# Taking twelve matmuls whose results nobody reads out of the routing of a mixture of experts

## The reference

```
def moe_ffn(h, router_w, w1, w3, w2):
    logits = (h @ router_w).astype(jnp.float32)
    vals, idx = lax.top_k(logits, TOP_K_EXPERTS)
    probs = jax.nn.softmax(vals, axis=-1)
    gate = jnp.sum(jax.nn.one_hot(idx, N_EXPERTS, dtype=jnp.float32) * probs[..., None], axis=-2)
    gate = gate.astype(h.dtype)
    out = jnp.zeros_like(h)
    for e in range(N_EXPERTS):
        out = out + gate[..., e:e + 1] * swiglu(h, w1[e], w3[e], w2[e])
    return out
```

## Time and profile before

| what | value |
|---|---|
| median of 3 runs | 1699.44 us (1698.66 to 1702.03) |
| the profiled execution's own time | 1701.22 us |
| its span | 1699.4 us |
| mean granted TensorE clock of the span | 0.988 |
| TensorE busy | 1638.2 us (96%), 8944 matmuls |
| VectorE busy | 1373.6 us (81%) |
| ScalarE busy | 1072.0 us (63%) |
| HBM read | 473.40 MB, 283 GB/s over the span |

### The profile page before, as it was taken

One profiled execution on the slowest core, in us unless ns is written; L12 is line 12 of the kernel. 1 busy time (PEld: TensorE's weight loads), 2 busy tenths in 40 slices (PEclk: granted clock), 3 DMA queues, 4 the chain that ended last, 5 costly groups with the idle time before them and its releaser, 6 DMA issues.

```text
span 1699.4 us, 24355 instructions
## 1 busy us (share of the span) xinstructions
PE 1638.2 (96%) x8944; PEld 1389.6 (82%) x8944; DVE 1373.6 (81%) x1140; ACT 1072.0 (63%) x896; POOL 458.4 (27%) x541
## 2 busy tenths in 40 slices
PE   7899998999999999999999999999999999999998
PEld 5787888989989788878888888888888888888786
DVE  6999675455669976688888888888888888888887
ACT  6345455444455554577777777777777777777774
POOL 8996801999142541233000000000000000000100
PEclk9899999999999999999999999999999999999999
DMA  8343555556544455489999999999999999999994
GB/s 315 122 156 120 173 192 189 186 168 227 166 151 149 149 162 176 139 300 391 369 378 378 370 367 388 365 386 382 365 374 378 373 385 376 360 380 370 385 395 180
DMA packets 212460, 481.58 MB, mean 283 GB/s; under 512 B 7936, under 2 KB 32640, under 8 KB 212144
## 3 DMA queue, kind: packets, MB, share of 16 engines
q1 hardware_dynamic: 207456, 463.34, 76.3%
q0 software_dynamic: 4512, 16.78, 2.7%
q10 hardware_dynamic: 432, 0.65, 0.1%
HBM read 473.40 MB, written 7.34 MB: 283 GB/s over the span
## 4 chain that ended last, share of the span: by engine, by line
PE 65%; DVE 4%; ACT 1%; DMA 1%; issue 1%; DVEq 0%; ACTq 0%
PE ps L649 19%; PE ps L651 19%; PE ps L650 19%; PE ps L1257 1%; DVE w_lo L281 1%; DMA raw<-moe_w 1%; PE ps L673 1%; PE ps L674 1%; PE ps L675 1%; PE ps L848 0%; ACT w_hi L276 0%; PE ps L1305 0%; DVE hid L2331 0%; DVE x_tok L2545 0%; PE ps L1210 0%
## 5 line engine op out<-in xcount | busy, mean ns | idle before, releaser
L281 DVE TENSOR_TENSOR w_lo<-raw,w_hi 128x2048 fp32r<-128x2048 f32 (+1 forms) x439 | 1013.1, 2318 | 239.2 <-ACT w_hi L276 237.7
L276 ACT ACTIVATE w_hi<-raw 128x2048 fp32r<-128x2048 f32 (+1 forms) x439 | 840.0, 1915 | 378.1 <-PE ps L651 285.7
L649 PE MATMUL ps<-w_hi,xg_hi 128*128 128x512 f32 x896 | 355.4, 397 | 0.8 <-DVE w_lo L281 0.8
L651 PE MATMUL ps<-w_hi,xg_lo 128*128 128x512 f32 x896 | 349.6, 390 | 0.0
L650 PE MATMUL ps<-w_lo,xg_hi 128*128 128x512 f32 x896 | 348.9, 389 | 0.0
L649 PE MATMUL ps<-w_hi,hidT_hi 128*128 128x512 f32 x528 | 207.5, 393 | 3.4 <-DVE hidT_lo L2345 1.8
L651 PE MATMUL ps<-w_hi,hidT_lo 128*128 128x512 f32 x528 | 206.4, 391 | 0.0
L650 PE MATMUL ps<-w_lo,hidT_hi 128*128 128x512 f32 x528 | 206.0, 390 | 0.0
L651 PEld LDWEIGHTS ps<-w_hi,xg_lo 128*128 128x128 f32 x896 | 168.2, 188 | 36.2
L649 PEld LDWEIGHTS ps<-w_hi,xg_hi 128*128 128x128 f32 x896 | 168.3, 188 | 35.2 <-issue 1.3
L650 PEld LDWEIGHTS ps<-w_lo,xg_hi 128*128 128x128 f32 x896 | 168.5, 188 | 33.3
(11 more groups left out here) (403 smaller groups left out, 2367.3 us busy)
## 6 DMA issues: line engine op xcount, KB each, us to landing
raw<-moe_w SPq DMA_DIRECT2D x336, 1024.0 KB, 7.2
raw<-w_in SPq DMA_DIRECT2D x44, 1024.0 KB, 5.5
raw<-ffn_w SPq DMA_DIRECT2D x33, 1024.0 KB, 5.3
raw<-w_o SPq DMA_DIRECT2D x8, 1024.0 KB, 5.2
raw<-w_out_a SPq DMA_DIRECT2D x4, 1024.0 KB, 5.1
raw<-w_out_c SPq DMA_DIRECT2D x4, 1024.0 KB, 5.7
raw<-w_out_b SPq DMA_DIRECT2D x4, 1024.0 KB, 5.2
raw<-w_in SPq DMA_DIRECT2D x4, 904.0 KB, 7.7
```

Source lines behind the costliest of these rows:

```text
L276: act.activation(w_hi[:, n % SPLIT, 0:width], raw[:, n % RAW, 0:width], ACT.Copy).then_inc(hi_done, 1)
L281: dve.tensor_tensor(w_lo[:, n % SPLIT, 0:width], raw[:, n % RAW, 0:width], w_hi[:, n % SPLIT, 0:width].bitcast(F32), ALU.subtract).then_in ...
L649: pe.matmul(dst, x_hi, hi, start=first, stop=False, skip_group_check=True)
L651: return pe.matmul(dst, x_lo, hi, start=False, stop=last, skip_group_check=True)
```

## The change

It takes away the helper `stay_awake` and both its calls, twelve matmuls with their weight loads. Nothing waited for them and nothing else is altered.

```
-                def stay_awake(times):
-
-                    for _ in range(times):
-                        pe.matmul(ps[:, 3, :], hT_hi[:, 0, 0:P], hT_hi[:, 0:2, :].rearrange("p k t -> p (k t)"),
-                                  start=True, stop=True, skip_group_check=True)
...
                 logits_of(1).then_inc(S["logits_ps"], 1)
-                stay_awake(8)
                 pe.wait_ge(S["triangle_done"], 2)
                 pe.wait_ge(S["picked"], 1)
...
                 pe.matmul(ps[:, 2, 16:24], ones_r[:, :], sel_r[:, 1, :], start=False, stop=True,
                           skip_group_check=True).then_inc(S["rank_ps"], 1)
-                stay_awake(4)
```

## The result

| | before | after |
|---|---|---|
| median | 1701.00 us (6 runs, 1698.66 to 1702.23) | 1706.48 us (6 runs, 1703.89 to 1707.39) |
| ratio | | 1.0031 (95% interval 1.0018 to 1.0043) |
| span of the profiled execution | 1699.4 us | 1705.1 us |
| granted clock of the span | 0.988 | 0.983 |

Without the twelve matmuls the kernel is slower, by 0.31%, or 5.3 us of 1701; the two medians lie 5.5 us apart. The runs of before are the three shown ahead of the prediction and three that were made beside the changed kernel; with them its median is 1.6 us higher.

The account below looks back on a forecast made before the run. It took TensorE's row and granted clock to bound the kernel. Terms -0.05 (helper), +3.07 (gather) and +1.2 (first chunk) summed to +4.2 us on 1699.44, giving 1703.6 us, range 1700.3 to 1705.8.

Parts of the forecast that it names:

- The idle stretch ahead of L1257: TensorE idle 1.61 us before turning `hid`: hides losses in chunks two to four, and would still be there.
- The base: Starting time the sum was added to: median of the runs shown, 1699.44 us.
- The first chunk, +1.2 us: Expert 0's first twelve matmuls run partly at clock 0.50: middle of bounds 0 and 2.4 us.
- The gather, +3.07 us: The gather's 32 matmuls at clock 0.50 take 6.83 us instead of 3.76; bounds 0 and 3.76 us more.
- The gain of 0.05 us: Routing, ahead of the gather: removing all twelve matmuls saves only 0.05 us, since VectorE's `h_lo` and `pick` cover them.
- The later part: Behind the first chunk: distances stay as before, counted 0; shortening by more than 0.7 us would mean being wrong.
- The early rise in the gather: Rival: clock rises during the gather, before 726, first chunk loses nothing; +1.6 us, 1701.0 us; chance 0.27.
- the twelve stood on the path: Rival: the helper's matmuls delayed the routing, up to 4.36 us go, 1695.1 us; chance 0.03.
- The late rise: Clock rises only behind the first chunk: +5.4 us, 1704.9 us; upper end of the main case, no own chance.
- the main case: Low clock through the gather and part of the first chunk: +3.1 to +5.4 us, 1702.5 to 1704.9; chance 0.70.

Follow-up runs that it names:

- the sixteen: Kernel before with sixteen helper matmuls instead of eight ahead of the rank matmuls, the four behind them kept: 1703.50 us, one execution, beside 1700.59.
- the eight alone: Kernel before with the helper's four matmuls behind the ranks left out, the eight ahead of them kept: 1703.01 us, ratio 1.0015.

## Why the prediction was right in kind and too small in size

**The direction and the mechanism held.** The loss is the half clock in the gather and the first chunk, and what is behind it moved along, as the prediction had it. The idle stretch ahead of L1257 was there again (2.03 us, 1.61 before) and hid nothing of the first chunk's loss, since it begins behind it.

**The measured time lies above the range**, 1706.48 us against 1705.8. Two steps failed. Of the 2.9 us between 1703.6 and 1706.48 the base has about 1.6, the first chunk's term 1.1 and the gather's 0.3; the larger gain takes 0.1 to 0.2 back.

*The base.* The step took the median of the three runs shown, 1699.44 us, against the profiled execution's own 1701.22. With more runs the kernel before has 1701.00 (6 runs), 1701.08 (20) and 1700.59 (21). The base was 1.1 to 1.6 us low, and the range, of which I gave 0.9 us at the top and 0.7 at the bottom to the spread of the runs, made too little room for it. Three runs between 1698.66 and 1702.03 were too few for a term of this size. On 1701.0 the same sum would have given 1705.2 us.

*The first chunk, +1.2 us.* The prediction's rows gave 2.8 and 3.5 us of wide matmuls at 0.50 ahead of a rise, +1.3 to +1.6 us, and it then took the middle between 0 and 2.4, since the gather "may count for a part". The chunk took 5.21 us on the chain (730.25 to 735.46) against 2.92, +2.3, nearly the upper bound: all twelve matmuls went at 0.50, for 5.2 us. That the gather would help was wrong: the run with matmuls of its shape shows no rise behind 24 of them and a whole gather. And the time to a rise is not fixed by the two rows: in the runs that entered the gather at 0.50 the clock came back 2.3 to 5.2 us after the chunk's start, and the chunk lost 0.7 to 2.1 us by its starts. What sets this from one execution to the next no run here shows.

*The gather, +3.07 us*, measured +3.33 (7.09 against 3.76 on the chain). Its pace was 0.2133 us as taken; the rest is a longer start. The prediction had set this term against the rule of the Trainium skill, page "TensorE: Matmul & The Clock Gate", section "LDWEIGHTS (loading the stationary operand)", by which it would be zero. The trace differs from that rule once more: the gather's loads are recorded with a median of 333 ns, and 192 ns before.

*The gain of 0.05 us* was 0.17 to 0.2 us. VectorE began on the ranks 722.21 - 721.01 = 1.20 us after `h_lo`'s start, before 721.19 - 719.83 = 1.36, so the ranks had come 0.16 us too late for it after all. To within that the cover was read rightly, and the sixteen show where it ends.

*The later part* was to shorten by no more than 0.7 us, and in the two profiled executions it shortened by 0.9. The prediction had made this a sign of being wrong. It is not one here, since the same part takes as little in the runs that lost nothing.

**The rivals.** The early rise in the gather (0.27) did not happen. Its evidence was transposes, behind which the clock came back in some traces only, and no gather shows a rise. That the twelve stood on the path (0.03) falls with 0.2 us. The late rise, which I had put into the main case as its upper end, is what happened in the profiled execution: -0.05 + 3.07 + 2.4 = +5.4 forecast, +5.42 to the turning of `hid`. That the two agree to the second digit is luck; the terms each differ by 0.1 to 0.3 us. Of the chances, slower had 0.57 and came.

## What to carry to other kernels

A stretch in the chain of waits is not yet a cost: here 4.36 us of matmuls stood in it and only 0.2 us could be gained, because VectorE's work ended at the same point. Before idle filler on TensorE is taken out, look at the granted clock on both sides of it and price the work behind it at the half clock, up to its upper bound. And where small matmuls let the clock fall, exchange their operands, so that the wide one streams. Here that gained 2.4 us on the kernel before for the same arithmetic, together with the filler; without the filler it lost 3.4. When a change is worth 0.3%, more than three runs of the kernel before are needed for the base.

## What the runs showed that I had not expected

- Of two kinds of instruction with the same 128 columns and nearly the same pace at half clock (sixteen in 3.3 to 3.5 us), sixteen float32 transposes brought the clock back in five of twelve places, and rounded-float32 matmuls in none of five whole gathers of 32.
- Eleven traces whose programs are the same up to the routing come to it with up to 4.6 us between them, nearly the whole effect of the change. A single execution's time says little here; the distances within the stretch that was changed say more.
- The clock can fall again within a few microseconds of its rise: with the eight alone it rose at 720.1 and was at 0.50 from 723.5 on, although TensorE worked without a break from 721.85.
- The router's matmuls at 8 result columns and 128 streamed ones ran 0.06 us apart and held the clock at 1.00 for as long as they ran, with only 8 of the array's columns giving results. I don't know from these runs whether it is the streamed columns alone that count.
